# Differential heads' values in pairs of column groups, and their norm by column-group sums and a spread in row groups

## What is computed

```python
def diff_mixer(q, k, v, pos, lq1, lk1, lq2, lk2, subln, lambda_init):
...
        p = jax.nn.softmax(sc, axis=-1)
        a = (p[:, 0] - lam * p[:, 1]).astype(v.dtype)
        return jnp.einsum('bhqk,bkhd->bqhd', a, v)
    o = sweep_query_blocks(block, q, pos)
    o = rmsnorm(o, subln) * (1.0 - lambda_init)
    return o.reshape(b, s, DIFF_HEADS * 2 * DIFF_HEAD_DIM)
```

## Time and profile before

| | |
|---|---|
| median of 3 runs | 1457.62 us (1457.6 to 1457.7) |
| profiled execution | 1457.46 us |
| its span | 1455.5 us |
| PE, DVE, ACT, POOL busy | 99%, 73%, 54%, 2% |
| granted clock of TensorE | 1.00 in every slice |

### The profile page before, as it was taken

One profiled execution on the slowest core, in us unless ns is written; L12 is line 12 of the kernel. 1 busy time (PEld: TensorE's weight loads), 2 busy tenths in 40 slices (PEclk: granted clock), 3 DMA queues, 4 the chain that ended last, 5 costly groups with the idle time before them and its releaser, 6 DMA issues.

```text
span 1455.5 us, 28504 instructions
## 1 busy us (share of the span) xinstructions
PE 1447.2 (99%) x12414; PEld 1403.4 (96%) x12414; DVE 1057.0 (73%) x1462; ACT 783.2 (54%) x1012; POOL 34.9 (2%) x41
## 2 busy tenths in 40 slices
PE   9999999999999999999999999999999999999999
PEld 9999998999999999999999899999999999989978
DVE  7766676897876655766548689888787799766844
ACT  6444555565554443544446566555645645775753
POOL 0000000210000000000000020000000000000000
PEclk9999999999999999999999999999999999999999
DMA  8655545444555555555554544466555454425541
GB/s 331 225 186 191 191 149 207 145 146 154 194 196 193 201 183 197 200 188 190 201 186 140 194 147 149 170 220 219 203 191 187 149 188 157 145 97 177 198 141 59
DMA packets 38843, 261.36 MB, mean 180 GB/s; under 512 B 4672, under 2 KB 5184, under 8 KB 9152
## 3 DMA queue, kind: packets, MB, share of 16 engines
q1 hardware_dynamic: 38576, 259.54, 52.4%
q10 hardware_dynamic: 144, 0.00, 0.0%
HBM read 258.48 MB, written 1.05 MB: 178 GB/s over the span
## 4 chain that ended last, share of the span: by engine, by line
PE 93%; DVE 6%; issue 1%; ACT 0%; POOL 0%; POOLq 0%
PE ps L257 29%; PE ps L258 28%; PE ps L259 28%; DVE w_low L231 2%; PE ps L1518 1%; DVE scratch L2226 1%; PE ps L1509 0%; PE ps L1491 0%; DVE even_s_rot L2228 0%; PE ps L1533 0%; DVE even_s_rot L2229 0%; DVE even_s_rot L2216 0%; DVE even_s_rot L2217 0%; PE ps L923 0%; PE ps L2812 0%
## 5 line engine op out<-in xcount | busy, mean ns | idle before, releaser
L224 ACT ACTIVATE w_high<-w_raw 128x2048 fp32r<-128x2048 f32 (+1 forms) x243 | 457.3, 1883 | 472.1 <-PE ps L259 469.0
L231 DVE TENSOR_TENSOR w_low<-w_raw,w_high 128x2048 fp32r<-128x2048 f32 (+1 forms) x240 | 545.3, 2273 | 203.2 <-ACT w_high L224 202.8
L257 PE MATMUL ps<-x,w_high 128*128 128x256 f32 x2224 | 622.4, 280 | 0.5 <-DVE w_low L231 0.4
L259 PE MATMUL ps<-x,w_low 128*128 128x256 f32 x2224 | 616.9, 277 | 0.0
L258 PE MATMUL ps<-x,w_high 128*128 128x256 f32 x2224 | 616.7, 277 | 0.0
L257 PEld LDWEIGHTS ps<-x,w_high 128*128 128x128 f32 x2224 | 418.3, 188 | 5.0 <-issue 3.3
L259 PEld LDWEIGHTS ps<-x,w_low 128*128 128x128 f32 x2224 | 418.8, 188 | 0.0
L258 PEld LDWEIGHTS ps<-x,w_high 128*128 128x128 f32 x2224 | 418.5, 188 | 0.3
L257 PE MATMUL ps<-ffn_hid,w_high 128*128 128x256 f32 x528 | 145.7, 276 | 0.0
L258 PE MATMUL ps<-ffn_hid,w_high 128*128 128x256 f32 x528 | 145.7, 276 | 0.0
L259 PE MATMUL ps<-ffn_hid,w_low 128*128 128x256 f32 x528 | 145.7, 276 | 0.0
(11 more groups left out here) (478 smaller groups left out, 2086.7 us busy)
## 6 DMA issues: line engine op xcount, KB each, us to landing
w_raw<-in_weights SPq DMA_DIRECT2D x229, 1024.0 KB, 4.9
w_raw<-in_weights SPq DMA_DIRECT2D x10, 768.0 KB, 4.2
setup_first<-in_first SPq DMA_DIRECT2D x8, 256.0 KB, 4.9
w_raw<-in_weights SPq DMA_DIRECT2D x4, 512.0 KB, 5.0
even_second_vectors<-in_second SPq DMA_DIRECT2D x1, 1836.0 KB, 7.4
w_raw<-in_weights SPq DMA_DIRECT2D x2, 640.0 KB, 3.9
resid<-in_x SPq DMA_DIRECT2D x1, 1024.0 KB, 10.7
out<-resid SPq DMA_DIRECT2D x3, 256.0 KB, 3.0
```

The costliest lines, as they stand in the source:

```text
L224: act.activation(self.slot(self.wh, n)[:, f], self.slot(self.raw, n)[:, f], ACT.Copy).then_inc(self.hi_made, 1)
L231: dve.tensor_tensor(self.slot(self.wl, n), self.slot(self.raw, n), self.slot(self.wh, n).bitcast(F32), ALU.subtract).then_inc(self.lo_made, 1)
L257: pe.matmul(out, ah, bh, start=start, stop=False, skip_group_check=True)
L259: return pe.matmul(out, al, bh, start=False, stop=stop, skip_group_check=True)
```

## The change

Values of differential heads are made as those of the latent heads, two heads at each odd a, features on partitions. The norm's sum over 64 features is then a sum over half of the partitions: four matmuls, one for each pair of heads, each with a 32-column stationary operand of ones (`half_sums`) in its own column group. The root and the reciprocal are taken of a 128x256 tile, and four matmuls (`half_spread`, 32 rows each, in its own row group, each into its own bank) spread them back over the partitions. VectorE multiplies outputs, spread factors and gain in one instruction; the eight transposes and the two scaled copies on ScalarE are gone. The filler grows by the 32 columns of two tensors that go.

```diff
@@ scalar
+        def diff_square(p):
+            act.wait_ge(*t["o_read"](HEADS // 2 + p + 1))
+            act.activation(m.dq[:, p, :], od[:, p, :], ACT.Square).then_inc(t["d_sq"].sem, 1)
...
+            if a >= HEADS + 4 and a % 2 == 0:
+                diff_square((a - HEADS - 4) // 2)
         tanh(S_BRANCH - 1)
+        diff_square(3)
 
         act.wait_ge(*t["pool_y"](4))
         act.activation(m.ph[:, :, :], m.pp[:, :, PAD:], ACT.Copy).then_inc(t["pool_h"].sem, 1)
...
             if n == S_BRANCH:
-                act.wait_ge(*t["o_read"](HEADS // 2 + HEADS))
-                act.activation(m.dq[:, :, :].rearrange("p a t -> p (a t)"),
-                               od[:, :, :, :].rearrange("p a h d -> p (a h d)"), ACT.Square).then_inc(t["d_sq"].sem, 1)
                 act.preload_act_table(ACT.Sqrt)
                 act.wait_ge(*t["d_ms"](1))
-                act.activation(m.drt[:, :], m.dms[:, :], ACT.Sqrt, bias=c.eps[:, 0:1], scale=1.0 / (2 * DH)).then_inc(t["d_rt"].sem, 1)
+                act.activation(self.diff_root(), c.bank(B_SUMS, SEQ), ACT.Sqrt, bias=c.eps[:, 0:1], scale=1.0 / (2 * DH)).then_inc(t["d_rt"].sem, 1)
...
             if n == S_BRANCH + 1:
-                act.wait_ge(*t["lam_made"](2))
-                act.wait_ge(*t["d_t"](1))
-                for i in range(2):
-                    act.activation(m.dk[:, 2 * i:2 * i + 2, :], c.halves(B_T + i), ACT.Copy,
-                                   scale=m.subl[:, 0:1]).then_inc(t["d_y"].sem, 1)
-                act.wait_ge(*t["d_y"](2))
+                act.wait_ge(*t["d_y"](1))
                 act.activation(m.yh[:, 4:8, :], m.dk[:, :, :], ACT.Copy).then_inc(t["d_h"].sem, 1)
@@ vector
         def take_out(a):
+            if a % 2 == 0:
+                return
...
-                dve.tensor_copy(od[:, :, a - HEADS, :], c.bank(B_O, P).rearrange("p (a d) -> p a d", a=2)).then_inc(t["o_read"].sem, 1)
+                dve.tensor_copy(od[:, p - HEADS // 2, :], c.bank(B_O, SEQ)).then_inc(t["o_read"].sem, 1)
+        def halves():
+            sums, spread, ones = self.half_sums(), self.half_spread(), m.bias[:, 0, QUAD:QUAD + 2]
+            for i in range(2):
+                rows = slice(P // 2 * i, P // 2 * i + P // 2)
+                for x in range(2):
+                    dve.memset(sums[rows, QUAD // 2 * x:QUAD // 2 * x + QUAD // 2], float(i == x))
+            firsts = c.tab[:, T_IDENT:T_IDENT + P].rearrange("p (g two i) -> p two i g", two=2, i=QUAD // 2)[:, :, 0, :]
+            ln(dve.tensor_reduce(ones, firsts, AX.X, ALU.add))
+            dve.tensor_copy(spread.rearrange("p (two f) -> p two f", two=2),
+                            ones.unsqueeze(2).to_broadcast([P, 2, P // 2])).then_inc(t["d_halves"].sem, 1)
...
             if a == 2 * HEADS:
+                halves()
                 dve.wait_ge(*t["pool_w"](1))
...
-            if n == S_BRANCH:
-                dve.wait_ge(*t["d_sq"](1))
-                dve.tensor_reduce(m.dms[:, :], m.dq[:, :, :].rearrange("p a (g d) -> p (a g) d", d=2 * DH), AX.X,
-                                  ALU.add).then_inc(t["d_ms"].sem, 1)
...
+                if n == S_BRANCH and part == 0:
+                    dve.wait_ge(*t["d_rt"](1))
+                    dve.reciprocal(self.diff_root(), self.diff_root()).then_inc(t["d_n"].sem, 1)
...
-            if n == S_BRANCH:
-                dve.wait_ge(*t["d_rt"](1))
-                ln(dve.reciprocal(m.drt[:, :], m.drt[:, :]))
-                o3 = od[:, :, :, :].rearrange("p a h d -> p (a h) d")
-                dve.tensor_tensor(o3, o3, m.drt[:, :].unsqueeze(2).to_broadcast([P, 16, 2 * DH]), ALU.mult).then_inc(t["d_n"].sem, 1)
+            if n == S_BRANCH + 1:
+                dve.wait_ge(*t["d_wide"](1))
+                dve.scalar_tensor_tensor(out=m.dk[:, :, :], in0=od, scalar=m.subl[:, 0:1], in1=c.ps[:, B_SPREAD:B_SPREAD + 4, 0:SEQ],
+                                         op0=ALU.mult, op1=ALU.mult).then_inc(t["d_y"].sem, 1)
@@ tensor
-        def times_v(a):
...
+        def diff_sums():
+            pe.wait_ge(*t["d_halves"](1))
+            pe.wait_ge(*t["d_sq"](4))
+            for p in range(4):
+                mm = pe.matmul(c.bank(B_SUMS, SEQ)[QUAD * p:QUAD * p + QUAD, :], self.half_sums(), m.dq[:, p, :], start=True,
+                               stop=True, skip_group_check=True)
+            mm.then_inc(t["d_ms"].sem, 1)
+        def diff_spread():
+            pe.wait_ge(*t["d_n"](1))
+            pe.wait_ge(*t["pool_y"](4))
+            pe.wait_ge(*t["turned_copied"](2 * HEADS))
+            pe.wait_ge(*t["o_read"](HEADS))
+            for p in range(4):
+                r = slice(QUAD * p, QUAD * p + QUAD)
+                mm = pe.matmul(c.bank(B_SPREAD + p, SEQ), self.half_spread()[r, :], self.diff_root()[r, :], start=True, stop=True)
+            mm.then_inc(t["d_wide"].sem, 1)
...
-            if a >= HEADS + 2:
-                times_v(a - 2)
-            elif a % 2 and a >= 3:
+            if a % 2 and a >= 3:
                 pair_values((a - 3) // 2)
...
-            if n == S_BRANCH + 1:
-                pe.wait_ge(*t["d_n"](1))
...
-                        mm = pe.transpose(c.halves(B_T + f // 2)[:, f % 2, x * P:(x + 1) * P],
-                                          od[:, x, 2 * f:2 * f + 2, :].rearrange("p h d -> p (h d)"), ident)
-                mm.then_inc(t["d_t"].sem, 1)
+                if n in (S_BRANCH, S_BRANCH + 1) and part == 0:
+                    (diff_sums if n == S_BRANCH else diff_spread)()
```

More of the change, by code:

```diff
@@ L971 @@
 GATE_ORDER = (2, 0, 1)
-B_S, B_POOL, B_T, B_O = 2, 4, 6, 7
+B_S, B_POOL, B_T, B_O, B_SUMS, B_SPREAD = 2, 4, 6, 7, 3, 4
 UNITS = ([(n, 0, "dve") for n in range(S_UQ)] + [(S_UQ, p, "act") for p in range(3)]
@@ L1018 @@
     scored=16, scores_read=16, max_made=16, exped=16, probs_made=16, turned=16, turned_copied=16, pv_done=16, o_high=4,
-    o_read=12, bias_made=8, lam_sum=1, lam_exp=1, lam_made=2, pool_zero=3, pool_step=4, pool_avg=4, pool_w=1, pool_y=4,
-    pool_h=1, pool_l=1, gated=S_BRANCH - S_GATE, d_sq=1, d_ms=1, d_rt=1, d_n=1, d_t=1, d_y=2, d_h=1, d_l=1, merged=8, merged_high=4,
+    o_read=8, bias_made=8, lam_sum=1, lam_exp=1, lam_made=2, pool_zero=3, pool_step=4, pool_avg=4, pool_w=1, pool_y=4,
+    pool_h=1, pool_l=1, gated=S_BRANCH - S_GATE, d_halves=1, d_sq=4, d_ms=1, d_rt=1, d_n=1, d_wide=1, d_y=1, d_h=1, d_l=1, merged=8, merged_high=4,
     merged_low=4)
@@ L1038, in __init__ @@
         self.nlam, self.subl = sb("neg_lam", [P, 1]), sb("subl", [P, 1])
-        self.dms, self.drt = sb("diff_ms", [P, 16]), sb("diff_rt", [P, 16])
-        self.room = sb("room", [P, 40])
+        self.room = sb("room", [P, 72])
         self.yh, self.yl = sb("y_high", [P, 8, SEQ], F32R), sb("y_low", [P, 8, SEQ], F32R)
@@ L1056, in filled, with half_sums, half_spread, diff_root @@
         return self.c.done, self.units + u + 1
+    def half_sums(self):
+        return self.m.bias[:, 0, 0:QUAD]
+    def half_spread(self):
+        return self.m.bias[:, 1, 0:P]
+    def diff_root(self):
+        return self.m.arena[:, 0, :]
     def gate(self, b, i):
@@ L1101, in scalar @@
         cqh, kvh = m.yh[:, 4:6], m.yh[:, 6:7]
-        od = m.v[:, :, :].rearrange("p t (h d) -> p t h d", h=HEADS)
+        od = m.v[:, :, :].rearrange("p t (a n) -> p (t a) n", n=SEQ)
         def after(n):
@@ L1312, in take_out @@
         def take_out(a):
+            if a % 2 == 0:
+                return
+            p = a // 2
             if a < HEADS:
-                if a % 2 == 0:
-                    return
-                p = a // 2
                 dve.wait_ge(*t["o_high"](p + 1))
@@ L1529, in pair_values @@
                     h = 2 * p + i
-                    d = slice(h * VD, h * VD + VD)
+                    v, d = (m.v, m.dv)[h // HEADS], slice(h % HEADS * VD, h % HEADS * VD + VD)
                     o, w = c.bank(B_O, SEQ)[64 * i:64 * i + 64, :], m.pt[:, i, :]
                     if tile == 0:
-                        pe.matmul(o, m.v[:, 0, d], w[:, 0:SEQ], start=True, stop=False, skip_group_check=True)
+                        pe.matmul(o, v[:, 0, d], w[:, 0:SEQ], start=True, stop=False, skip_group_check=True)
                     else:
-                        pe.matmul(o[:, P:SEQ], m.v[:, 1, d], w[:, SEQ:3 * P], start=False, stop=True,
+                        pe.matmul(o[:, P:SEQ], v[:, 1, d], w[:, SEQ:3 * P], start=False, stop=True,
                                   skip_group_check=True).then_inc(t["pv_done"].sem, 1)
-        def times_v(a):
[L1539 to L1547, removed]
+        def diff_sums():
[14 more added lines that the diff above has]
+            mm.then_inc(t["d_wide"].sem, 1)
         def out_part(n, kks):
@@ L1661, in tensor @@
                 mm.then_inc(c.done, 1)
-            if n == S_BRANCH + 1:
-                pe.wait_ge(*t["d_n"](1))
-                pe.wait_ge(*t["turned_copied"](2 * HEADS))
-                for f in range(4):
-                    for x in range(2):
```

(5 more changed lines are left out.)

## The result

| | before | after |
|---|---|---|
| median, 6 runs each | 1457.61 us | 1462.99 us |
| lowest to highest | 1457.01 to 1458.11 | 1461.63 to 1463.62 |
| profiled execution | 1457.46 us | 1462.38 us |
| its span | 1455.5 us | 1460.5 us |

The ratio is 1.0038, with a 95% interval of 1.0027 to 1.0048: slower by 5.4 us, by more than 0.2%. The forecast was 1458.8 us, in a range of 1455.8 to 1461.8. The time is outside of it, and next to the 1462.9 of rival 2.

The account below looks back on a forecast made before the run. TensorE, busy 1447.2 of 1455.5 us, was taken as the bound. Its own work (-1.5) and the stall (+2.9) gave +1.4, less 0.2 for pace: 1458.7 profiled, 1458.8 us median, range 1455.8 to 1461.8.

Parts of the forecast that it names:

- rival 2: Long stream behind the spread falls to the slower pace: 480 matmuls, 4.1 us in both mixers, 1462.9 us; chance 0.10.
- the one on the pace: TensorE's streams: two paces, about 0.1178 and 0.1135 us a matmul, seemingly settled at the insertion ahead; not derived.
- a gain in slots 24 and 25: Half of these slots' matmuls might take the faster pace, 0.4 us; half of that was counted.
- the loop's streams: Streams of slots 17 to 23 in the differential-head loop: forecast difference 0.
- the stall: Inside slot 24, TensorE's sums wait for the last pair's square: 1.45 us a mixer, 2.9 in both, bounds 1.2 to 2.0.
- `halves`: Six small VectorE instructions at a = 16, about 1 us in all, with 1.2 us of cover remaining.
- own work: TensorE's insertions, added less removed: -0.735 us a mixer, -1.5 for two, between -2.5 and -0.3 with bounds.
- Values: Value insertions in the differential-head loop, per mixer: 5.32 us removed, 3.98 added.
- The steps out: Leaving row or column groups for the stream: 0.10 us, priced into the sums and the spread.
- my case: Stall of 1.2 to 2 and own work as summed: 1457.4 to 1460.3 us, chance 0.68.
- second wait: At the spread, TensorE waits for VectorE's reciprocal: ready near 355.0, asked for at 356.7, so 1.7 us of cover.
- The clock: Risk that the 1.45 us standstill halves TensorE's clock: 24 matmuls at 1.2 GHz cost 3 us more; chance 0.03.

Follow-up runs that it names:

- e1: Changed kernel with VectorE's copy of the last pair put ahead of the low part of slot 26: 1460.77 us, ratio 1.0019.
- e2: Changed kernel with the split weights of slot 26 placed 24 columns lower: 1460.22 us, ratio 1.0015.
- e8: Changed kernel with VectorE's last copy ahead of slot 26's low part, and slot 25's split weights placed 24 columns lower: 1456.47 us, ratio 0.9994.
- e7: Changed kernel with the spread behind part 1 of slot 25 and three full-array transposes behind the spread: 1460.37 us, ratio 1.0019.
- e4: Changed kernel with the spread moved behind part 1 of slot 25, where the transposes stood: 1463.75 us, ratio 1.0038.
- e5: Kernel before with the split weights of slot 26 placed 24 columns lower: 1457.53 us, ratio 1.0002.
- e6: Kernel before with three matmuls in row groups put behind its transposes: 1459.06 us, ratio 1.0011.
- e3: Changed kernel with VectorE's last copy ahead of slot 26's low part, and slot 26's split weights placed 24 columns lower: 1456.99 us, ratio 0.9992.

## Why the prediction was wrong

**The step that failed** is the one on the pace: "Which pace a stream takes seems settled at the insertion ahead of it, and I can't derive it." The sum nevertheless took the long stream as staying fast, and even 0.2 us as a gain in slots 24 and 25. Slot 24's second part and slot 25's first did run fast after the sums (48 in 5.66 us), a gain of the kind that I counted; but of the 480 behind the spread the last 456, fast before, were slow: 456 by 0.0045, 2.05 us a mixer. With slots 24 and 25 the pace cost 3.7 us in both mixers where the sum had -0.2. That is rival 2, at a price near its own (4.1 us, 1462.9 us). It had 0.10, with no row on either side that decided; and the range was cut at 1461.8, short of it. Its count was misread: it takes 24 matmuls of slot 25 as fast before, but the transposes stood behind slot 25, and all 96 of slots 24 and 25 were slow. That its 1462.9 comes within 0.1 us of the median is partly luck: the loop's streams cost 1.0 us more, and 1.0 us was gained in unchanged code. The experiments show its cause only as far as this: it is TensorE's own (nobody is waited for, the clock is 1.00), it is not the stall's (e1), and it can be turned by the weights' place (e2, e8) or by what is inserted ahead of it (e7 against e4).

**The stall was right** in place, cause and size: forecast 1.45 a mixer, shown as 1.44 and worth 1.52 by e1. The chain is the one that was read: low part of slot 26, copy, square. `halves` took 0.6 us, not 1, and was covered.

**The own work was right**, a little better than priced. By the prediction's own measure the sums took 0.765 us without the wait (forecast 0.76; 348.49 less 347.49 less 0.235, in e1) and the spread 0.835 (forecast 0.74; 355.59 less 354.52 less 0.235). Values came out at -1.56 instead of -1.34. The steps into both insertions took 0.21 and 0.20 us, where full-array insertions are entered in 0.12 or 0.13 (344.88 to 345.00, 356.85 to 356.98 before). The steps out took 0.22, which the prediction also put down to the change of groups; but the second step behind full-array transposes is 0.21 as well (357.77 to 357.98 before), so leaving groups costs 0.01 or 0.02 us more, not 0.10. The Trainium skill ("TensorEngine Tiling (Array Packing)", Key Properties) says that a change of the tiling mode drains TensorE; the trace agrees with it for the way in, and hardly shows it for the way out.

**The loop's streams** lost 0.51 a mixer, which the sum had as zero. Before, slots 17, 21 and 23 were fast, after it only 23. It is no accident of one execution: slots 17 and 21 are fast in both mixers of the three traces with the old values (before, e5, e6), and in the ten with the new ones and the loop's weights unmoved slots 17 to 22 are slow in 19 mixers of 20 (the other is the second of e3). It is the same unknown in small, and no rival had it with this sign.

**Two bounds were summed wrongly.** The upper end of TensorE's own work by its own terms is -0.15 us, not -0.3, and "my case" with all its bounds is 1457.3 to 1461.3 us, not up to 1460.3. The measured time is above that too.

**No second wait** came, as forecast: the reciprocal took 1.75 us, from 351.12, and TensorE asked for it at 354.72. The clock did not move: with TensorE standing for 1.44 us, the granted clock stayed 1.00 in the windows behind it. The rule of the Trainium skill ("TensorE: Matmul & The Clock Gate", The HAM clock gate) that idle time takes the clock down, weighed as a risk, did not come to bear on a gap of this length.

What the change is worth without its two side costs is what e3 and e8 show: about 1 us less than the kernel before in their medians, which is not more than these runs can tell from nothing (upper ends 1.0001 and 1.0003). The loop's slower streams (1.0 us) are still in it. The forecast own-work gain of 1.5 us agrees with it and is not shown by it.

**Left open**: what selects the pace when a stream is entered. It is not tried whether the four matmuls of the spread, exactly, would slow the kernel before, nor what other operands than the weights do when they are moved.

## What to carry to other kernels

Where one engine is busy for 99% of the time, its step in a long steady stream is a term of the sum like any other: multiply it out first (here 456 matmuls by 0.0045 us by two) and give a rival that large a chance that fits what is not known, whatever the edit's own work is. After any edit ahead of such a stream, compare starts of its matmuls, not only waits. If the step has changed, moving the weights of one slot is a cheap trial (e8: one constant, 4 us). Look for the other pace in the trace that you have, too: here it showed what ends a slow stream before anything was run. An operation that is moved to a place between two parts of a stream turns its whole chain of producers into cover that must be counted; here the order of one copy on VectorE was worth 1.5 us a mixer.

## What was not expected of the hardware

The same matmul (128x128 weights, 256 columns, rounded operands) ran in streams at three steady steps, 0.1133, 0.1178 and 0.1200 us behind the first few, all at a granted clock of 1.00 and with no wait shown. A step holds over hundreds of matmuls and ten slots of weights. Slot 13 of the first mixer has two of them in two executions; its first matmul and the next insertion, in the changed kernel:

```profile
267.10 0.36 PE L257 MATMUL ps<-x,w_high 128*128 128x256 f32 x1
...
272.85 0.27 PE L1536 MATMUL ps<-table,mix_probs 128*128 128x128 f32 x1
```

and in e1, whose edit comes into play only at a = 17, behind it:

```profile
268.02 0.37 PE L257 MATMUL ps<-x,w_high 128*128 128x256 f32 x1
...
273.56 0.49 PE L1538 MATMUL ps<-table,mix_probs 128*128 128x128 f32 x3
```

5.75 and 5.54 us for 48 matmuls: same code so far, same operands at the same places, same insertion ahead, other step. So neither the program's operands nor the insertion alone decide; something that differs from one execution to the next, such as the moment of entry, does as well. (Slot 13 of the second mixer would not show this: its weights lie in another of the three buffers of the ring.) A passage from slow to fast was seen in the middle of a stream (e2, e8, and slot 2 of the next stage before), each time at a slot whose weights lie 24 columns lower. In the long streams of the mixers none went back.
